# Attention: the inverse row sums of a tile are spread over partitions through a DRAM scratch row instead of by matrix products

## The reference

```python
for i in range(lp // BLOCK):
    q0, kend = i * BLOCK, (i + 1) * BLOCK
    s = jnp.einsum('bqhd,bkhd->bhqk', q[:, q0:kend], k[:, :kend]) * scale
    s = s + c[:, :, q0:kend, None] - c[:, :, None, :kend]
    ...
    p = jax.nn.softmax(jnp.where(mask[None, None], s, NEG_INF), axis=-1)
    outs.append(jnp.einsum('bhqk,bkhd->bqhd', p, v[:, :kend]))
```

## Time and profile before

| | us |
|---|---|
| median of 3 runs | 2929.63 |
| lowest, highest | 2927.26, 2930.67 |
| span of the profiled execution | 2924.8 |
| attention stage in it | 870 to 1354 |
| PE busy over the span | 2840.5 |
| DVE, ACT, POOL busy over the span | 1712.9, 616.3, 1350.4 |

### The profile page before, as it was taken

How to read it: one execution, slowest core, us unless ns; L and a number is a source line. 1 busy time by engine, 2 the same in 40 slices (tenths; PEclk the granted TensorE clock), 3 DMA queues, 4 the chain that set the end, 5 groups by cost and what they waited for, 6 DMA issues and landing times.

```text
span 2924.8 us, 40628 instructions
## 1 busy us (share of the span) xinstructions
PE 2840.5 (97%) x14442; PEld 2069.8 (71%) x14442; DVE 1712.9 (59%) x4617; ACT 616.3 (21%) x1269; POOL 1350.4 (46%) x1140
## 2 busy tenths in 40 slices
PE   8999999999999999998999989999999999999997
PEld 4478888888875555554455767878877777777775
DVE  6665656656346767674677534777677773332326
ACT  2221212110025454552110100011111111111114
POOL 3433534447730110101355335677667666555645
PEclk9999999999999999999999999999999999999999
DMA  6500110101121103014435456889989989999986
GB/s 219 184 6 1 31 45 1 30 15 44 30 77 35 63 30 129 28 33 170 173 137 159 131 198 197 270 277 277 271 277 289 291 271 302 305 304 305 317 258 254
DMA packets 192571, 470.49 MB, mean 161 GB/s; under 512 B 27384, under 2 KB 108104, under 8 KB 166632
## 3 DMA queue, kind: packets, MB, share of 16 engines
q1 hardware_dynamic: 145424, 347.63, 33.3%
q0 software_dynamic: 44640, 111.84, 16.5%
q10 hardware_dynamic: 2304, 8.39, 0.7%
HBM read 349.64 MB, written 118.11 MB: 160 GB/s over the span
## 4 chain that ended last, share of the span: by engine, by line
PE 39%; DMA 6%; DVE 3%; POOL 2%; issue 2%; SPq 1%; another core or an unknown queue 0%; ACT 0%; DVEq 0%; POOLq 0%; ACTq 0%
PE ps L3021 18%; PE ps L2796 6%; DMA moe_xg<-t_rows,index 5%; PE ps L2969 4%; PE ps L2940 3%; PE ps L2852 2%; DVE moe_xT L2097 2%; PE ps L2937 2%; POOL moe_xg L2523 1%; PE ps L2862 1%; PE ps L2815 1%; POOL moe_fin L2605 1%; PE ps L2806 0%; DMA base_rows<-moe_yo,index 0%
## 5 line engine op out<-in xcount | busy, mean ns | idle before, releaser
L2523 POOL DMA_INDIRECT moe_xg<-t_rows,index x433 | 428.6, 990 | 174.7 <-issue 139.2
L3021 PEld LDWEIGHTS ps<-moe_xT,moe_wg 128*128 128x128 f32 x2048 | 352.5, 196 | 54.6 <-issue 31.3
L3021 PE MATMUL ps<-moe_xT,moe_wg 128*128 128x192 f32 (+22 forms) x2048 | 380.0, 338 | 9.3 <-DVE moe_hh L1997 5.4
L3021 PE MATMUL ps<-moe_xT,moe_wu 128*128 128x192 f32 (+22 forms) x2048 | 376.3, 337 | 0.0
L3021 PEld LDWEIGHTS ps<-moe_xT,moe_wu 128*128 128x128 f32 x2048 | 354.2, 197 | 4.8
L2544 POOL DMA_INDIRECT base_rows<-moe_yo,index x100 | 231.0, 2310 | 273.2 <-DVE moe_yo L2111 116.8
L2097 DVE STREAM_TRANSPOSE moe_xT<-moe_xg 128x256 f32<-128x256 f32 x433 | 235.1, 610 | 174.2 <-DMA moe_xg<-t_rows,index 155.9
L1296 POOL TENSOR_TENSOR fox_diag<-fox_c,fox_causal 128x128 f32<-128x128 f32 x128 | 55.8, 457 | 450.9 <-DVE fox_mx L1325 446.1
L2660 ACT ACTIVATE moe_sl<-ps 128x256 f32<-128x256 f32 (+19 forms) x144 | 49.6, 345 | 953.9 <-PE ps L3021 736.8
L1997 DVE TENSOR_TENSOR moe_hh<-moe_sl,ps 128x256 f32<-128x256 f32 (+19 forms) x144 | 49.7, 358 | 292.4 <-ACT moe_sl L2660 194.9
L1319 DVE CUSTOM_DVE_ANT_0 hT<-ps,fox_c 128x512 f32<-128x512 f32 (+7 forms) x320 | 166.3, 560 | 63.0 <-PE ps L1581 62.7
(11 more groups left out here) (373 smaller groups left out, 5052.1 us busy)
## 6 DMA issues: line engine op xcount, KB each, us to landing
moe_wg<-in_we_gate SPq DMA_DIRECT2D x64, 1024.0 KB
moe_wu<-in_we_up SPq DMA_DIRECT2D x64, 1024.0 KB
moe_wd<-in_we_down SPq DMA_DIRECT2D x64, 1024.0 KB
fox_c<-ck SPq DMA_DIRECT2D x8, 1032.0 KB, 8.9
emb_xin<-in_x SPq DMA_DIRECT2D x16, 512.0 KB, 3.9
h_rows<-emb_hr SPq DMA_DIRECT2D x16, 512.0 KB, 2.7
ret_w<-in_w_in SPq DMA_DIRECT2D x16, 512.0 KB, 6.6
moe_yt<-h_rows SPq DMA_DIRECT2D x16, 512.0 KB
```

The costliest lines, as they stand in the source:

```text
L2523: pool.indirect_dma_start(out=xg[g % NXG][:, :], out_offset=None, in_=quarters, in_offset=bass.IndirectOffsetOnAxis(ap=route.index4[:, AT4 ...
L3021: ins = pe.matmul(out, w[:, c, f:FF:FC], xT[u][:, c, 0:n], start=(c == 0), stop=(c == DC - 1))
```

## The change

The products with diagonal matrices, the four multiplications that make them, the copy of their result by ACT and the matrix of ones go. In their place SP writes the four columns of inverses to a scratch row in DRAM (two rows in turn, 4 x 128 values), waits until they have landed, and reads them back twice, once for each head, each time repeated over 64 partitions. DVE's `finish` waits for both reads and for the last product.

```diff
+            def inverse_rows(n):
+                b = n % 2
+                sp.wait_ge(inverted, n + 1)
+                sp.dma_start(rinv_rows[b].rearrange("r k -> k r"), rinv[b][:, :], allow_slow_non_contiguous=True).then_inc(rinv_out, 16)
+                sp.wait_ge(rinv_out, 16 * (n + 1))
+                if n >= 2:
+                    sp.wait_ge(scaled, n - 1)
+                for a in range(2):
+                    sp.dma_start(rB[b][FD * a:FD * (a + 1), :].rearrange("p (q k) -> p q k", q=2),
+                                 rinv_rows[b].rearrange("(q a) k -> a q k", a=2)[a].partition_broadcast(FD)).then_inc(rB_in[b], 16)
...
             for n, (p, t) in enumerate(order):
+                inverse_rows(n)
...
-                sp.wait_ge(scaled, n + 1)
-                sp.dma_start(foxT[2 * FD * p:2 * FD * (p + 1), QT * t:QT * (t + 1)], oT[n % 2][:, :]).then_inc(o_s[n % 2], 16)
-                if (n + 1) % TILES == 0 and p + 2 < PAIRS:
-                    pair_values(p + 2)
-                    pair_gates(p + 2)
+                if n >= 1:
+                    store(n - 1)
+                if n >= 1 and n % TILES == 0 and p + 1 < PAIRS:
+                    pair_values(p + 1)
+                    pair_gates(p + 1)
+            store(NT - 1)
...
             def inverse(n):
                 b = n % 2
                 dve.wait_ge(exped, 4 * n + 4)
                 if n >= 2:
-
-                    dve.wait_ge(spread, n - 1)
+                    dve.wait_ge(rinv_out, 16 * (n - 1))
                 dve.reciprocal(rinv[b][:, :], rs[b][:, :]).then_inc(inverted, 1)
-                dve.wait_ge(inverted, n + 1)
-                for r in range(4):
-                    ins = dve.tensor_scalar(rd[b][:, r, :], ident[:, :], rinv[b][:, r:r + 1], None, ALU.mult)
-                ins.then_inc(rd_set, 1)
...
             def finish(n):
                 b = n % 2
-                dve.wait_ge(spread_c, n + 1)
+                dve.wait_ge(weighed, step0[n + 1])
+                dve.wait_ge(rB_in[b], 32 * (n // 2 + 1))
...
-            def keep(n):
-                b = n % 2
-                act.wait_ge(spread, n + 1)
-                if n >= 2:
-                    act.wait_ge(scaled, n - 1)
-                nc.scalar.copy(rB[b][:, :], ps[:, O0 + b, QT:2 * QT]).then_inc(spread_c, 1)
...
-            def scatter(n):
-                pe.wait_ge(rd_set, n + 1)
...
-                for q in range(2):
-                    for a in range(2):
-                        ins = pe.matmul(ps[FD * a:FD * (a + 1), O0 + n % 2, QT + P * q:QT + P * (q + 1)], onesf[:, :],
-                                        rd[n % 2][:, 2 * q + a, :], start=True, stop=True)
-                ins.then_inc(spread, 1)
```

More of the change, by code:

```diff
@@ L1104, in retention_phase, with fox_phase @@
         yield
-def fox_phase(nc, ps, ident, hT, square, w_in, w_out, v_rows, ck, mixed, mT_rows, foxT, ahead):
+def fox_phase(nc, ps, ident, hT, square, w_in, w_out, v_rows, ck, mixed, mT_rows, foxT, rinv_rows, ahead):
     with Phase(nc, "fox") as ph:
@@ L1186, in fox_phase @@
         pT = [sb(f"pT{b}", [P, 4, P]) for b in range(4)]
-        rd = [sb(f"rd{b}", [P, 4, P]) for b in range(2)]
         rB = [sb(f"rB{b}", [P, QT]) for b in range(2)]
@@ L1190, in fox_phase @@
         zero = lambda name: ph.zero_sems(name, 1)[0]
-        tab, ones_set = ahead.fox_tab, zero("ones_set")
+        tab = ahead.fox_tab
         w_s, v_s, c_s = ahead.fox_w, ahead.fox_v, ahead.fox_c
@@ L1203, in fox_phase @@
         turned, pT_a, pT_d, weighed = (zero(n) for n in ("turned", "pT_a", "pT_d", "weighed"))
-        inverted, rd_set, spread, spread_c, scaled = (zero(n) for n in ("inverted", "rd_set", "spread", "spread_c", "scaled"))
+        inverted, rinv_out, scaled = (zero(n) for n in ("inverted", "rinv_out", "scaled"))
+        rB_in = ph.zero_sems("rB_in", 2)
         block = yield
@@ L1262, in _, with store @@
             pair_gates(1)
+            def inverse_rows(n):
[8 more added lines that the diff above has]
+                                 rinv_rows[b].rearrange("(q a) k -> a q k", a=2)[a].partition_broadcast(FD)).then_inc(rB_in[b], 16)
+            def store(n):
+                p, t = order[n]
+                sp.wait_ge(scaled, n + 1)
+                sp.dma_start(foxT[2 * FD * p:2 * FD * (p + 1), QT * t:QT * (t + 1)], oT[n % 2][:, :]).then_inc(o_s[n % 2], 16)
             for n, (p, t) in enumerate(order):
+                inverse_rows(n)
                 if n in TURN_AT:
@@ L1516, in _ @@
                         exps(n + 1, q, a)
-                    if i == 0 and n >= 1:
-                        keep(n - 1)
-            keep(NT - 1)
         @block.tensor
@@ L1673, in _ @@
                         scores(n + 1, u)
-                if early:
-                    scatter(n)
-                else:
-                    if order[n][1] == 0:
-                        for s in after:
-                            turn(n + 1, s)
-                        scatter(n)
-                    else:
-                        scatter(n)
-                        for u in (range(first[n + 2]) if n + 2 < NT else []):
-                            scores(n + 2, u)
-                        for s in after:
-                            turn(n + 1, s)
+                if not early:
+                    for u in (range(first[n + 2]) if n + 2 < NT and order[n][1] else []):
+                        scores(n + 2, u)
+                    for s in after:
+                        turn(n + 1, s)
         yield
@@ L3075, in build @@
     mixed, foxT = dram("mixed", (SEQ, RH * RD)), dram("foxT", (FH * FD, SEQ))
-    mT_rows = dram("mT_rows", (NX, P, RH * P))
+    mT_rows, rinv_rows = dram("mT_rows", (NX, P, RH * P)), dram("rinv_rows", (2, 4, P))
     t_rows, base_rows = dram("t_rows", (SEQ + SPARE, D)), dram("base_rows", (SEQ + SPARE, D))
@@ L3086, in build @@
                   retention_phase(nc, ps, ident, hT, a["square"], a["w_in"], a["retc"], v_rows, ck, mixed, ahead),
-                  fox_phase(nc, ps, ident, hT, a["square"], a["w_in"], a["w_out"], v_rows, ck, mixed, mT_rows, foxT, ahead)]
+                  fox_phase(nc, ps, ident, hT, a["square"], a["w_in"], a["w_out"], v_rows, ck, mixed, mT_rows, foxT, rinv_rows, ahead)]
         for stage in stages:
```

4 lines of the change are left out of this document (removed).

## The result

The kernel before takes 2928.45 us in the runs beside the changed one (2926.21 to 2930.67), the changed kernel 2962.77 us (2959.08 to 2965.37). The ratio is 1.0112, with an interval of 1.0096 to 1.0127: slower by 1.1%, some 34 us, where 9 us less were forecast. The profiled execution has a span of 2963.4 us, 38.6 us above that of before.

The account below looks back on a forecast made before the run. PE, busy 97% of the span, was taken as the bound. Removed products were to give 11.3 us and the uncovered end to cost 2.1, so -9.2 us from 2929.6, taken as 2920.5 us; range 2911 to 2929.

Parts of the forecast that it names:

- x: In each tile's chain: cost of writing 512 runs of 4 bytes beyond an ordinary transfer, 1.5 us, between 0 and 4.9.
- The rest of the chain: Each tile, after the write: 0.5 us to issue the second read, 1.9 for the read, 0.2 for two wake-ups.
- The rule on small runs: Scratch write: one descriptor per element, a 19-fold loss, would make it some 36 us; no run showed it.
- the tile behind values and gates: Tile t = 6, write queued behind 3 MB: chain of 19 us under 30.1 us of cover, cost 0.
- turned rows and stores: On SP's queue behind its new waits: each wanted an iteration or two later, so no cost counted.
- the signs named for a wrong forecast: DVE waiting for a transfer at t = 7 or 1; PE's ACT waits growing over 5 us; a landing above 9 us.
- The end: Behind the last tile nothing covers the chain: last finish late by 0.6 + x, 2.1 us, between 0.6 and 5.5.
- The rival for the slow write: Chains outlast the tiles' cover, deciding from about 13.4 us; 20 us slower, 2950 us, at 15 us; chance 0.11.
- PE's gain: Attention stage: of 19.5 us of removed products 11.3 return, 2.95 per full pair, 2.5 in the last.
- eaten by waits: Rival: PE, ahead by 0.5 us a tile, meets ACT's exponentials; half of 11.3 us left, 2926 us; chance 0.22.
- All of it comes back: Rival: all 19.5 us of PE and up to 2 from DVE are gained, 2910 to 2912 us; chance 0.15.
- The hidden chain: All tiles but the last: a transfer chain of 6.0 us lies beneath 13.2 us or more from reciprocal to finish, cost 0.

Follow-up runs that it names:

- e2: Changed kernel with only two of the four inverse columns written (256 runs of 4 bytes), each read back for both query blocks: 2959.54 us, single run.
- p1: Kernel as e1, plus nine kinds of small transfers issued singly behind the attention stage's last store: 128, 256 and 512 neighbouring single-value writes took 8.3 to 8.4 us.
- e3: Changed kernel with SP's order altered: write first, then turned rows and store, then wait and reads, bulk last: 2959.39 us, ratio 1.0099 to before.
- e4: Changed kernel with the last two tiles scaled by diagonal-matrix products as before, the other 30 through DRAM: 2946.5 us, ratio 1.0058 to before.
- s1: As e1, but tiles 8 and 9 written in 512 runs of 4 bytes: 2909.26 us against 2913.73 before, ratio 0.9978.
- e1: Changed kernel with inverses written as 128 runs of 16 bytes, so values return in wrong order: 2924.04 us against 2927.52 before, ratio 0.9993.
- c3: As c1, but the last tile scaled by diagonal-matrix products as before: 2905.98 us against 2913.73 before, ratio 0.9969.
- c1: Changed kernel with inverses turned on DVE in 32x32 blocks, four writes of 4 runs of 128 bytes: 2909.2 us against 2913.73 before, ratio 0.998.

## Why the prediction was wrong

**The step that failed first is x**, what the write of single values costs beyond an ordinary transfer. It was taken as 1.5 us, with 4.9 as its upper bound. The write took 8.0 us on a quiet queue against the 1.9 of an ordinary one, so x is 6.1 us, above the bound. The rest of the chain was too small too: 3.5 us from the issue of the reads to the finish, where 0.5 + 1.9 us and a wake-up had been taken. The bound was scaled from a load of 1024 runs of 32 bytes by the number of runs. e2 and p1 show that between 128 and 512 this number has no say (the same 8.3 to 8.4 us), and that loads tell nothing of it (512 single values read: 2.6 us; written: 8.4 us). The row was near in size of run and far in kind.

**The rule on small runs** of the Trainium skill ("DMA: Bandwidth & Descriptors", section "Rules for kernel authors") was right in its sign. The page gives its 19-fold loss for a transpose by a rearranged access pattern against the hardware's own transpose, and not for a small write; carried over to it as an estimate of 36 us, it was too much. Measured here, 8.4 against 1.4 us is 6 times. That each element is a transfer of its own, the trace confirms (528 packets for 512 values), but 512 of them with distance between them take 2.7 us, twice the ordinary time. One descriptor per element is not by itself what makes this write slow.

**The second failed step is that each chain was priced from its own reciprocal, on an idle queue.** With 12 us the chain is still below the 13.4 us from which the rival let it decide, and in the first pair that holds: not one finish waits. The losses come where the chain meets something else. For the tile behind values and gates I had 19 us, a backlog of 13 and a chain of 6, against 30.1 us of cover. The write and reads took 15.7 + 3.7 us, near those 19, but by luck: the bulk added some 8 us and not 13, and the slow write made up for it. What the step left out is the wait before the write. SP was still in the chain of the tile before, whose reciprocal comes 3.5 us earlier, and issued the write 13.1 us late, so that `finish` came after 32.5 us. In the third pair the three chains of tiles 17 to 19 begin 14 to 17 us late in this way. I had written that turned rows and stores behind SP's waits are wanted an iteration or two later; DVE waited for turned rows 7 times, 10.9 us in all, and e3 shows that with these rows sent first the finishes wait longer instead. Of the signs named for a wrong forecast these came: a wait of DVE at t = 1 (2.5 us in the third pair), a landing above 9 us (15.7), and PE's waits for ACT at the turns, which grew by more than 5 us (34.7 to 42.6).

**The clock** was in no step. The rival priced a stall at its length. In the changed kernel the clock fell to 0.50 four times in the stage, and 10.9 us of work were lost that way, about as much as the 11.3 us that PE was to gain. In the execution of e4, with the same work up to tile 29, it was 3.9 us, and s1, where the stall is shorter, has none of it in the pairs.

**The end** was put at +2.1 us, and 0.6 + x by the same formula would give 6.7 us with the measured x. It came to 16 us: 20.0 us between last reciprocal and last finish against 4.0. The formula has one chain, and there are two in a row, since the reciprocals of t = 1 and t = 0 of the last pair stand 6.2 us apart (1362.50 and 1368.68) and the two chains took 13.8 and 13.9 us, with writes of 10.2 and 10.4. The rival for the slow write has the same gap: its 9.5 us at a chain of 13.5 are one chain less the 4.0 of before. e4, which does the last two tiles by products, gives back 16.3 us. Two stores stood behind the last reciprocal before the change as well (L1273, twice from 1350.69 on); only the chain is new there.

**PE's gain** was nearly right. Of 11.3 us forecast, 8.1 came, read where nothing disturbs it, at e1's last reciprocal. Up to there PE was busy 11.9 us less than before (444.7 against 456.6) and idle 3.8 us more (25.0 against 21.2). A full pair gave 2.0 to 2.1 us, not 2.95. Between long tiles the step gets shorter by 0.3 us, not 0.5. From the weighting L1625 at 1031.26 to the scores at 1034.25 were 2.99 us before:

```profile
1031.26 0.44 PE L1625 MATMUL ps<-fox_pT,fox_v 128*64 128x128 f32 x4
...
1034.25 0.94 PE L1581 MATMUL ps<-fox_qk 64*128 64x400 f32 x4
```

In e1 it is 2.67:

```profile
1028.52 0.44 PE L1629 MATMUL ps<-fox_pT,fox_v 128*64 128x128 f32 x4
1028.63 0.69 DVE L1366 COPY fox_pT<-ps 128x512 f32<-128x512 f32 x1 [2.68 <-PE ps L1604]
1028.89 1.21 PE L1604 MATMUL ps<-ident,hT 128*128 128x128 f32 x8
...
1030.03 1.23 PE L1629 MATMUL ps<-fox_pT,fox_v 16*64 16x256 f32 x8
...
1031.19 1.37 PE L1585 MATMUL ps<-fox_qk 64*128 64x400 f32 x6
```

The turns start at once, as worked out, but the eight now take 1.21 us instead of 1.09, since their second group needs the bank that DVE's copy leaves at 1029.32. The rival "eaten by waits" describes this in small. "All of it comes back" is refuted, also by c3.

**The hidden chain** was right for a chain of the size that was forecast. In e1 the median write lands after 1.8 us and the reads after 2.7, and DVE waits for the values only at the very end; its end costs 1.9 us more than before, where 2.1 was forecast. That these agree is partly luck: the last write took 2.3 us where 3.4 were reckoned, and the reads 3.5 where 2.4 and a wake-up were. The mechanism of the forecast holds with a write of ordinary speed. Its size does not come out as clearly: e1's time is 3.5 us below before, with an interval from 5.6 less to 1.2 more, where 9.2 less was forecast. The change has another mechanism.

**The chances.** The slow write had 0.11, with "beyond the upper bound" as the argument against it. A bound drawn from one row of another kind should not have carried that much.

## What to carry to other kernels

Values that are sent through DRAM to change their layout should be written in whole runs. Runs of 16 bytes a partition were fast enough here, but leave the values in another order; turning them on chip first gives runs of 128 bytes and the right order. Whether the reordering could be left to the read is not shown: 512 single values are read in 2.6 us, but no kernel here reorders in the read that repeats them over 64 partitions. A chain of transfers that must wait on an in-order queue is to be priced where it meets bulk and where two chains meet, not in a quiet tile, and the last tile, which nothing covers, is better done on chip (4.07 us against 6.1 in the traces of c3 and c1). A stall in a stage bound by PE may cost more than its length, because the clock can fall after it.

## What the runs showed of the hardware

Single values of 4 bytes written side by side to DRAM from different partitions take 8.1 to 8.4 us when nothing else is under way, whether 128, 256 or 512 of them. 16 take 1.3, 32 take 4.3, 64 take 6.9 us. At distances of 8, 16 and 32 bytes 128 values take 2.8, 2.1 and 1.4 us. Side by side, 128 runs of 8 bytes take 3.1 and of 16 bytes 1.4 us. 512 single values side by side are read in 2.6 us.

Behind 3 or 4 MB on the same queue a write takes 6 to 8 us more: 14.6 to 16.2 us in single values, 8.1 to 9.7 in runs of 16 bytes. On another queue beside the same bulk it took 13.6 us.

A small write from SBUF in good form lands 1.3 to 1.4 us after its issue, below the 1.9 us that I had taken as the floor from 128 KB transfers.

The granted clock fell to 0.50 after PE had idled 1.9 us of three (at 1043), and stayed at 1.00 where it idled 0.8 us of three (s1, at 1043) and where it idled 2.2 us of three (e4, at 1230). While PE idled at the end of the changed kernel's stage (from 1375 to 1391) it is 0.50 as well. The shortest of the four stretches was some 4 us long, the longest about 10.

What decides between a fall and none, beyond these cases, stays open: e4 has a clock of 1.00 in the last pair, where the changed kernel fell once.
